# Spreading the first half's inverse roots by two rounded products in a gated convolution layer

## The chip, the cores and the metric

The kernel runs on one core of a Trainium2 chip. Its engines are TensorE (PE in the profile; PEld is its weight load), VectorE (DVE), ScalarE (ACT), GpSimd (POOL), and SyncE (SP), which issues most transfers. Each works through its own queue of instructions in order, and they wait for each other by semaphores. The metric is the device time of one execution in microseconds (us).

## What is computed

One layer with a convolutional mixer (the reference's list of layers has one entry): a sequence of 1024 rows with 1024 channels, all in float32.

```python
def rms_norm(x, g):
    xf = x.astype(jnp.float32)
    y = xf * lax.rsqrt(jnp.mean(xf * xf, axis=-1, keepdims=True) + RMS_EPS)
    return (y * g.astype(jnp.float32)).astype(x.dtype)

def conv_mixer(h, w_in, conv_w, conv_b, ln_g, ln_b, w_out):
    z = h @ w_in
    a, b, gate = jnp.split(z, 3, axis=-1)
    u = a * jax.nn.sigmoid(b)
    u = lax.conv_general_dilated(
        u, conv_w[:, None, :], window_strides=(1,), padding=[(CONV_K - 1, 0)],
        dimension_numbers=("NWC", "WIO", "NWC"), feature_group_count=CONV_WIDTH,
    ) + conv_b
    uf = u.astype(jnp.float32)
    mu = jnp.mean(uf, axis=-1, keepdims=True)
    var = jnp.mean(jnp.square(uf - mu), axis=-1, keepdims=True)
    uf = (uf - mu) * lax.rsqrt(var + LN_EPS) * ln_g.astype(jnp.float32) + ln_b.astype(jnp.float32)
    u = jax.nn.silu(uf).astype(h.dtype) * jax.nn.silu(gate)
    return u @ w_out

# the layer: h + conv_mixer(rms_norm(h, norm_g[0]), ...)
```

`1 / sqrt(mean(x*x) + eps)` of a row is what this text calls the row's inverse root.

## The kernel before

**Layout.** Activations lie with the channels on the 128 partitions (8 groups, index `k`) and the rows along the free axis. The 1024 rows are two halves of 512 (index `h`), each of four tiles of 128 (`TPH`); tiles 0 to 3 are the first half, 4 to 7 the second. The second half is worked on first. Each f32 value of a projection is split into a rounded part (`_hi`, type fp32r) and a remainder (`_lo`), and each product of the projection is three matmuls: hi by hi, lo by hi, hi by lo.

**Projection.** The 24 groups of output channels are "units" (`UNITS`: b and a of a group in turn, then the gate's g). A pass is one unit on one half: 8 `k` times 3 products of 512 columns, 24 in all. The order of passes (`PASSES`) is written out: units 0 and 1 run on raw x (scaled by `norm_g` only) for half 1 and then half 0; then unit 2 and unit 3 on half 0, the same two on half 1, and from unit 4 on each unit on both halves. Half 0 of units 2 and 3 still uses raw x. From unit 2 on half 1 the normalized x is used; its hi part comes from ScalarE (`split_x`, L810), its remainder from GpSimd (`finish_x_lo`, L1427). Behind the projection come the means and deviations of the normalization (L692, L702) and seven output products (L711).

**Inverse roots.** The inverse root of a row stands on the row's partition and has to lie along the free axis, the same on all partitions. ScalarE squares and sums a tile (`square`, L773); GpSimd makes the mean with eps (L1418) and raises it to -0.5 (L1421), for tiles 4 to 7 one at a time, for tiles 0 to 2 together and then tile 3. Then a diagonal matrix of the 128 values is made for each tile, and TensorE multiplies a matrix of ones with it (`spread_rms`). For the second half VectorE makes a rounded and a remainder diagonal for each tile in `diags` (L1086, L1089), and two products of 512 columns add up in one bank (L620, L622). For the first half ScalarE makes four f32 diagonals in `sgate` (`rms_diagonal`, L793), and four f32 products of 128 columns follow (L626). The spread of half 0 stands in unit 3 on half 0 in front of its third `k` (`SPREAD_AT[0] = (3, 0, 2)`).

**Who needs the spread.** ScalarE copies it to SBUF (`copy_rms`, L798), VectorE scales the first units with the copy and makes the normalized x from the spread itself (L1130, L1136, L1098).

**The queues around it.** The order in each queue is written by hand. On ScalarE: squares of tiles 0 to 3 among the splits, `split_x(1, 2)`, the four diagonals, `split_x(1, 3)`, `split_x(1, 4)`, `copy_rms(0)`. On GpSimd: the first weight remainder, two x remainders of half 1, the inverse roots of tiles 0 to 2 and of 3, six more x remainders, the sum of lanes (L1472), the remainder of unit 4's weights (L1438), eight x remainders of half 0, and then the convolution's sums. On VectorE a subtraction of unit 3's weights (L1120, both inputs in SBUF) stands between the normalized x of `k` 5 and 6.

## Time and profile before

| | us |
|---|---|
| median of three runs (363.17 to 363.48) | 363.22 |
| profiled execution, its own time | 363.72 |
| its span | 361.9 |
| TensorE busy | 356.9 |
| VectorE busy | 319.9 |
| GpSimd busy | 269.8 |
| ScalarE busy | 232.4 |

Times in the trace are counted from the start of the span. In a timeline row stand the start, the duration, the engine, the line of the kernel, the operation, what is written and read, and how many instructions are merged in the row; in square brackets the idle time of the engine in front of it and who ended it. Durations on TensorE overlap: products of 512 columns are recorded with 0.39 to 0.40 us each and start 0.23 us apart, so starts are compared, and not durations added up. The 128-column f32 products leave two records each.

### The profile page before, as it was taken

What the parts mean: (1) busy time and instruction counts of PE and PEld (TensorE: products, weight loads), DVE (VectorE), ACT (ScalarE), POOL (GpSimd) and SP (SyncE); (2) the same over time, 40 slices, a digit from 0 to 9 for tenths busy, and PEclk for the clock granted to TensorE, in tenths of its full rate; (3) what the DMA queues carried; (4) which work ended last, traced back from release to release, by engine and by line L of the source; (5) the groups of instructions that cost most, each with busy time, mean ns of one, the idle gap of its engine ahead of it and who ended that gap; (6) DMA issues with size and microseconds to landing.
All of it is one profiled execution on the core that took longest, in us unless ns stands there. A gap on an engine that the chain in (4) does not pass through costs nothing.

```text
span 361.9 us, 4758 instructions
## 1 busy us (share of the span) xinstructions
PE 356.9 (99%) x1564; PEld 289.2 (80%) x1564; DVE 319.9 (88%) x514; ACT 232.4 (64%) x334; POOL 269.8 (75%) x194
## 2 busy tenths in 40 slices
PE   7999999999999999999999999999999999999996
PEld 6888888888888888888888888888888888888885
DVE  4779799999999899999999998993798979997952
ACT  5889685558847772998667875975655951452400
POOL 0029999999999997899999999795796532359220
PEclk9999999999999999999999999999999999999999
DMA  7995011201411311406112214235713695066042
GB/s 260 403 400 206 34 60 58 91 28 58 116 60 53 65 60 58 116 2 116 58 60 51 67 58 80 96 58 103 246 59 117 237 404 173 0 203 205 31 169 92
DMA packets 30520, 43.51 MB, mean 120 GB/s; under 512 B 18336, under 2 KB 18848, under 8 KB 30496
## 3 DMA queue, kind: packets, MB, share of 16 engines
q1 hardware_dynamic: 30352, 43.21, 37.7%
q8 instruction: 12, 0.20, 0.2%
q14 instruction: 12, 0.10, 0.1%
q10 hardware_dynamic: 144, 0.00, 0.0%
HBM read 34.82 MB, written 4.19 MB: 108 GB/s over the span
## 4 chain that ended last, share of the span: by engine, by line
PE 97%; DMA 1%; SPq 0%; ACT 0%; DVE 0%; issue 0%
PE mm L632 68%; PE acc L711 12%; PE mm L711 9%; PE mm L649 6%; DMA raw<-w_in 1%; PE acc L702 0%; PE acc L692 0%; PE acc L626 0%; ACT w_hi L786 0%; DVE nat L1273 0%; SPq L494 0%; SPq L520 0%; PE acc L620 0%; PE acc L622 0%
## 5 line engine op out<-in xcount | busy, mean ns | idle before, releaser
L632 PE MATMUL mm<-x_hi,w_hi 128*128 128x512 f32 x352 | 139.3, 396 | 0.0
L632 PE MATMUL mm<-x_hi,w_lo 128*128 128x512 f32 x352 | 139.0, 395 | 0.0
L632 PE MATMUL mm<-x_lo,w_hi 128*128 128x512 f32 x352 | 139.0, 395 | 0.0
L1185 DVE SCALAR_TENSOR_TENSOR acc<-u,chan,acc 128x512 f32<-128x512 f32 x157 | 110.7, 750 | 0.1
L632 PEld LDWEIGHTS mm<-x_hi,w_lo 128*128 128x128 f32 x352 | 66.1, 188 | 16.0
L632 PEld LDWEIGHTS mm<-x_hi,w_hi 128*128 128x128 f32 x352 | 66.1, 188 | 15.8
L632 PEld LDWEIGHTS mm<-x_lo,w_hi 128*128 128x128 f32 x352 | 66.1, 188 | 15.8
L1494 POOL TENSOR_TENSOR pconv<-pconv,prod 128x512 f32<-128x512 f32 x60 | 77.3, 1312 | 1.3 <-ACT prod L868 1.3
L1185 DVE SCALAR_TENSOR_TENSOR acc<-u,w_sum,acc 128x512 f32<-128x512 f32 x90 | 67.5, 750 | 1.3 <-ACT acc L850 1.1
L868 ACT ACTIVATE prod<-u,chan 128x512 f32<-128x512 f32 x69 | 47.7, 714 | 15.6 <-POOL pconv L1494 14.3
L1438 POOL TENSOR_TENSOR w_lo<-raw,w_hi 128x1024 fp32r<-128x1024 f32 (+1 forms) x21 | 49.7, 2365 | 9.3 <-ACT w_hi L817 9.2
L1494 POOL TENSOR_TENSOR pool_before<-pool_before,prod 128x512 f32<-128x512 f32 x37 | 48.3, 1305 | 1.1
L951 ACT ACTIVATE x_hi<-sgate 128x512 fp32r<-128x512 f32 x28 | 15.9, 624 | 18.2 <-DVE sgate L1261 18.2
L1454 POOL TENSOR_TENSOR wb_lo<-raw,wb_hi 128x1024 fp32r<-128x1024 f32 x6 | 14.5, 2418 | 16.8 <-DVE x_lo L1241 11.4
L711 PE MATMUL acc<-wb_hi,x_lo 128*128 128x512 f32 (+1 forms) x68 | 26.0, 382 | 0.0
L711 PE MATMUL acc<-wb_lo,x_hi 128*128 128x512 f32 (+1 forms) x68 | 25.9, 382 | 0.0
L711 PE MATMUL acc<-wb_hi,x_hi 128*128 128x512 f32 (+1 forms) x68 | 25.9, 382 | 0.0
L868 ACT ACTIVATE prod<-u,w_sum 128x512 f32<-128x512 f32 x30 | 21.4, 714 | 6.6 <-POOL pool_before L1494 6.6
L817 ACT ACTIVATE w_hi<-raw 128x1024 fp32r<-128x1024 f32 x22 | 23.0, 1047 | 2.7 <-PE mm L632 2.1
L1273 DVE TENSOR_TENSOR nat<-acc,nat 128x512 f32<-128x512 f32 (+1 forms) x22 | 13.7, 660 | 8.9 <-PE acc L711 8.9
L894 ACT ACTIVATE sgate<-nat 128x1024 uint16<-128x1024 uint16 x14 | 14.0, 1046 | 11.8 <-POOL nat L1485 8.7
L907 ACT ACTIVATE rows<-sgate 128x1024 uint16<-128x1024 uint16 x14 | 18.2, 1372 | 4.1 <-DMA sgate<-sgate 3.4
(109 smaller groups left out, 541.2 us busy)
## 6 DMA issues: line engine op xcount, KB each, us to landing
raw<-w_in SPq DMA_DIRECT2D x22, 512.0 KB, 3.3
nat<-x_t SPq DMA_DIRECT2D x16, 256.0 KB, 6.1
sgate<-x SPq DMA_DIRECT2D x8, 512.0 KB, 10.8
raw<-w_out SPq DMA_DIRECT2D x8, 512.0 KB, 3.3
nat<-x SPq DMA_DIRECT2D x8, 512.0 KB, 7.9
y<-nat SPq DMA_DIRECT2D x15, 256.0 KB, 2.1
raw_late<-w_out SPq DMA_DIRECT2D x4, 512.0 KB, 4.1
sig<-w_out SPq DMA_DIRECT2D x4, 512.0 KB, 3.9
```

What stands on the lines that cost most here:

```text
L632: ins = nc.tensor.matmul(bank(("unit", m, h)), w[:, m % 3, k, :], xx[:, k, half(h)], start=(k == 0 and i == 0), stop=(k == KC - 1 and i == 2))
L649: return nc.tensor.matmul(bank(("unit", m, h)), w[:, m, k, :], xx[:, k, half(h)], start=(k == 0 and i == 0), stop=(k == KC - 1 and i == 2))
L711: ins = nc.tensor.matmul(product_bank(b, q), v[:, k0 + k, rows], w[:, k, piece_columns(b, q)], start=(k == 0 and i == 0 and continued(b, q ...
L817: nc.scalar.activation(w_hi[:, m % 3, :, :].rearrange("p k n -> p (k n)"), raw[:, m % 2, :], ACT.Copy).then_inc(whi_ready, 1)
L868: nc.scalar.activation(dst, chain_in(j, chain, k), ACT.Identity, scale=tap(j, chain, k), bias=bias(j, chain) if k == 0 else 0.0).then_inc( ...
L894: nc.scalar.activation(planes()[:, i * T:(i + 1) * T].rearrange("p (h s q) -> p h s q", h=NH, s=2), words(nat[:, j, :])[:, :, i].rearrange ...
L907: nc.scalar.activation(words_of_rows(side)[:, :, :, i], crossed()[:, NT * i:NT * (i + 1), :], ACT.Copy).then_inc(rows_joined, 1)
L951: nc.scalar.activation(v_pair(b, k)[0], v_raw(b, k), ACT.Copy).then_inc(vhi_ready, 1)
L1185: ins = nc.vector.scalar_tensor_tensor(dst, chain_in(j, chain, k), tap(j, chain, k), chain_bank(j, chain), ALU.mult, ALU.add)
L1438: nc.gpsimd.tensor_tensor(w_lo[:, m % 3, ks, :].rearrange("p k n -> p (k n)"), raw[:, m % 2, ks.start * P:], w_hi[:, m % 3, ks, :].rearran ...
L1454: ins = nc.gpsimd.tensor_tensor(lo, source, hi.bitcast(F32), ALU.subtract)
L1494: ins = nc.gpsimd.tensor_tensor(pool_sum(chain), summand, prod[:, SLOTTED.index((j, chain, k)) % 4, :], ALU.add)
```

## The change

The first half's inverse roots are treated as the second half's are. GpSimd rounds them to fp32r and subtracts the rounded from the full value (`split_rms`, new, once for tiles 0 to 2 and once for tile 3). ScalarE makes from each part a diagonal, so eight instead of four, and writes them to `diags`, which the second half's spread has used before (hence the wait on `rms_all_ready`). TensorE waits for all eight and issues two products of 512 columns with the rounded ones. The old wait was for each diagonal in turn.

```diff
+        rms_parts = sb("rms_parts", [P, 2, TPH], F32R)
...
-        def diag(i):
-
-            return sgate[:, i, 0:P]
-
...
             def spread_rms(h):

+                spread = rms_spread(h).rearrange("p (t q) -> p t q", t=TPH)
+                pe.wait_ge(ones_r_ready, 1)
                 if h == 1:
-                    spread = rms_spread(1).rearrange("p (t q) -> p t q", t=TPH)
-                    pe.wait_ge(ones_r_ready, 1)
                     pe.wait_ge(diag_hi_ready, TPH)
-                    nc.tensor.matmul(spread, ones_r[:], diags[:, 0, :, :], start=True, stop=False)
+                else:
+                    pe.wait_ge(diag_ready, 2 * TPH)
+                nc.tensor.matmul(spread, ones_r[:], diags[:, 0, :, :], start=True, stop=False)
+                if h == 1:
                     pe.wait_ge(diag_lo_ready, TPH)
-                    ins = nc.tensor.matmul(spread, ones_r[:], diags[:, 1, :, :], start=False, stop=True)
-                else:
-                    for i in range(TPH):
-                        pe.wait_ge(diag_ready, i + 1)
-                        ins = nc.tensor.matmul(rms_spread(0)[:, i * P:(i + 1) * P], ones[:], diag(i), start=True, stop=True)
-                ins.then_inc(rms_all_ready, 1)
+                nc.tensor.matmul(spread, ones_r[:], diags[:, 1, :, :], start=False, stop=True).then_inc(rms_all_ready, 1)
...
             def rms_diagonal(t):

                 act.wait_ge(ident_in, 16)
-                act.wait_ge(rms_ready, rms_count(t))
-                nc.scalar.activation(diag(t), ident[:], ACT.Copy, scale=rms[:, t:t + 1]).then_inc(diag_ready, 1)
+                act.wait_ge(rms_all_ready, 1)
+                for i in range(2):
+                    act.wait_ge(rms_parts_ready, 2 * (rms_count(t) - TPH - 1) + i + 1)
+                    nc.scalar.activation(diags[:, i, t, :], ident[:], ACT.Copy,
+                                         scale=rms_parts[:, i, t:t + 1].bitcast(F32)).then_inc(diag_ready, 1)
...
+            def split_rms(tiles):
+
+                part = slice(tiles[0], tiles[-1] + 1)
+                done = 2 * (rms_count(tiles[0]) - TPH - 1)
+                pool.wait_ge(rms_ready, rms_count(tiles[0]))
+                nc.gpsimd.tensor_scalar(rms_parts[:, 0, part], rms[:, part], 1.0, 0.0, ALU.mult,
+                                        ALU.add).then_inc(rms_parts_ready, 1)
+                pool.wait_ge(rms_parts_ready, done + 1)
+                nc.gpsimd.tensor_tensor(rms_parts[:, 1, part], rms[:, part], rms_parts[:, 0, part].bitcast(F32),
+                                        ALU.subtract).then_inc(rms_parts_ready, 1)
+
...
             inverse_rms(range(TPH - 1))
+            split_rms(range(TPH - 1))
             inverse_rms((TPH - 1,))
+            split_rms((TPH - 1,))
```

On GpSimd, between the x remainders (L1427) and the next six of them, the queue before reads:

```order
L1427 TENSOR_TENSOR x_lo<-nat,x_hi 128x512 [waits xhi_ready] x2
L1418 TENSOR_SCALAR mean_sq<-mean_sq 128x3 [waits sumsq_ready]
L1421 TENSOR_TENSOR rms<-mean_sq,half_neg 128x3 [waits ms_ready]
L1418 TENSOR_SCALAR mean_sq<-mean_sq 128x1 [waits sumsq_ready]
L1421 TENSOR_TENSOR rms<-mean_sq,half_neg 128x1 [waits ms_ready]
L1427 TENSOR_TENSOR x_lo<-nat,x_hi 128x512 [waits xhi_ready] x6
```

The same place in GpSimd's queue now, with the line numbers of the changed kernel:

```order
L1437 TENSOR_TENSOR x_lo<-nat,x_hi 128x512 [waits xhi_ready] x2
L1417 TENSOR_SCALAR mean_sq<-mean_sq 128x3 [waits sumsq_ready]
L1420 TENSOR_TENSOR rms<-mean_sq,half_neg 128x3 [waits ms_ready]
L1428 TENSOR_SCALAR rms_parts<-rms 128x3 [waits rms_ready]
L1431 TENSOR_TENSOR rms_parts<-rms,rms_parts 128x3 [waits rms_parts_ready]
L1417 TENSOR_SCALAR mean_sq<-mean_sq 128x1 [waits sumsq_ready]
L1420 TENSOR_TENSOR rms<-mean_sq,half_neg 128x1 [waits ms_ready]
L1428 TENSOR_SCALAR rms_parts<-rms 128x1 [waits rms_ready]
L1431 TENSOR_TENSOR rms_parts<-rms,rms_parts 128x1 [waits rms_parts_ready]
L1437 TENSOR_TENSOR x_lo<-nat,x_hi 128x512 [waits xhi_ready] x6
```

Four small steps are added, two behind each power, and the six x remainders stand behind them.

On ScalarE, from the third `split_x` (L810) to the copy of the spread (L798), the queue before reads:

```order
L810 ACTIVATE x_hi<-nat 128x512 [waits a_ready,hn_ready]
L793 ACTIVATE sgate<-ident,rms 128x128 [waits rms_ready,ident_in] x4
L810 ACTIVATE x_hi<-nat 128x512 [waits a_ready,hn_ready] x2
L798 ACTIVATE pconv<-acc 128x512 [waits rms_all_ready]
L810 ACTIVATE x_hi<-nat 128x512 [waits a_ready,hn_ready]
```

The same place on ScalarE now (L791 is the diagonal):

```order
L809 ACTIVATE x_hi<-nat 128x512 [waits a_ready,hn_ready]
L791 ACTIVATE diags<-ident,rms_parts 128x128 [waits rms_parts_ready,rms_all_ready,ident_in]
L791 ACTIVATE diags<-ident,rms_parts 128x128 [waits rms_parts_ready]
...
L791 ACTIVATE diags<-ident,rms_parts 128x128 [waits rms_parts_ready,rms_all_ready,ident_in]
L791 ACTIVATE diags<-ident,rms_parts 128x128 [waits rms_parts_ready]
L809 ACTIVATE x_hi<-nat 128x512 [waits a_ready,hn_ready] x2
L797 ACTIVATE pconv<-acc 128x512 [waits rms_all_ready]
```

Eight diagonals stand where four stood, and each waits for its part; the two splits and the copy come behind all eight.

## Rows read from the trace of the kernel before

**Rows 1.** The page, parts 1, 2 and 4: busy time, granted clock, last chain.
```profile
PE 356.9 (99%) x1564; PEld 289.2 (80%) x1564; DVE 319.9 (88%) x514; ACT 232.4 (64%) x334; POOL 269.8 (75%) x194
...
PEclk9999999999999999999999999999999999999999
...
PE 97%; DMA 1%; SPq 0%; ACT 0%; DVE 0%; issue 0%
```

**Rows 2.** Waits of TensorE: us in total, times, longest.
```profile
PE mm L649 <- ACT w_hi L786: 1.2, 1, 1.2
```

**Rows 3.** Timeline of TensorE at the first half's spread: start, duration, instruction.
```profile
36.77 1.05 PE L626 MATMUL acc<-sgate,ones 128*128 128x128 f32 x8
37.58 0.47 PE L632 MATMUL mm<-x_hi,w_hi 128*128 128x512 f32 x1
37.89 0.39 PE L632 MATMUL mm<-x_lo,w_hi 128*128 128x512 f32 x1
```

**Rows 4.** Timeline of TensorE at the second half's spread.
```profile
25.12 0.39 PE L620 MATMUL acc<-diags,ones_r 128*128 128x512 f32 x1
...
25.58 0.40 PE L649 MATMUL mm<-x_hi,w_hi 128*128 128x512 f32 x1
```

**Rows 5.** Timeline of ScalarE, from the diagonals to the copy.
```profile
34.09 1.31 ACT L793 ACTIVATE sgate<-ident,rms 128x128 f32<-128x128 f32 x4
35.31 1.14 ACT L810 ACTIVATE x_hi<-nat 128x512 fp32r<-128x512 f32 x2
37.86 0.60 ACT L798 ACTIVATE pconv<-acc 128x512 f32<-128x512 f32 x1 [1.41 <-PE acc L626]
```

**Rows 6.** Timeline of GpSimd, inverse roots of tiles 0 to 3.
```profile
32.40 0.19 POOL L1418 TENSOR_SCALAR mean_sq<-mean_sq 128x3 f32<-128x3 f32 x1
32.68 0.85 POOL L1421 TENSOR_TENSOR rms<-mean_sq,half_neg 128x3 f32<-128x3 f32 x1
33.75 0.53 POOL L1418 TENSOR_SCALAR mean_sq<-mean_sq 128x1 f32<-128x1 f32 x1 [0.22 <-ACT sgate L773]
34.36 0.55 POOL L1421 TENSOR_TENSOR rms<-mean_sq,half_neg 128x1 f32<-128x1 f32 x1
34.87 3.79 POOL L1427 TENSOR_TENSOR x_lo<-nat,x_hi 128x512 fp32r<-128x512 f32 x3
```

**Rows 7.** Timeline of VectorE beside it.
```profile
33.01 1.22 DVE L1120 TENSOR_TENSOR w_lo<-raw,w_hi 128x1024 fp32r<-128x1024 f32 x1
```

**Rows 8.** Groups of GpSimd by shape: count, busy us, mean ns of one.
```profile
L1438 POOL TENSOR_TENSOR w_lo<-raw,w_hi 128x1024 fp32r<-128x1024 f32 x20 | 48.4, 2418 | 9.3 <-ACT w_hi L817 9.2
...
L1427 POOL TENSOR_TENSOR x_lo<-nat,x_hi 128x512 fp32r<-128x512 f32 x16 | 20.3, 1296 | 0.6 <-ACT x_hi L810 0.6
```

**Rows 9.** Timelines of TensorE and ScalarE at TensorE's one wait.
```profile
7.33 0.50 PE L649 MATMUL mm<-x_hi,w_hi 128*128 128x512 f32 x1 [1.17 <-ACT w_hi L786]
7.67 0.62 PE L649 MATMUL mm<-x_lo,w_hi 128*128 128x512 f32 x2
...
6.65 0.63 ACT L786 ACTIVATE w_hi<-raw 128x512 fp32r<-128x512 f32 x1 [1.57 <-DMA raw<-w_in]
```

**Rows 10.** Timeline of GpSimd, weight remainders of unit 4 and of a later one.
```profile
44.49 2.41 POOL L1438 TENSOR_TENSOR w_lo<-raw,w_hi 128x1024 fp32r<-128x1024 f32 x1 [0.16 <-ACT w_hi L817]
...
145.41 2.41 POOL L1438 TENSOR_TENSOR w_lo<-raw,w_hi 128x1024 fp32r<-128x1024 f32 x1 [3.07 <-ACT w_hi L817]
```

**Rows 11.** Timelines of VectorE, ScalarE and the weight loads near the end.
```profile
259.95 4.87 DVE L1205 TENSOR_TENSOR nat<-nat,acc 128x512 f32<-128x512 f32 x8 [0.51 <-PE acc L692]
...
275.15 0.60 ACT L834 ACTIVATE sgate<-mm 128x512 f32<-128x512 f32 x1 [2.17 <-PE mm L632]
...
276.30 2.50 DVE L1241 TENSOR_TENSOR x_lo<-sgate,x_hi 128x512 fp32r<-128x512 f32 x4 [0.72 <-ACT x_hi L951]
...
285.21 2.49 DVE L1241 TENSOR_TENSOR x_lo<-sgate,x_hi 128x512 fp32r<-128x512 f32 x4
...
285.91 0.19 PEld L711 LDWEIGHTS mm<-wb_hi,x_hi 128*128 128x128 f32 x1
```

More of the change, by code:

```diff
@@ L203, in gated_conv_layer @@
         rms_all_ready = sem("rms_all_ready")
+        rms_parts_ready = sem("rms_parts_ready")
         hn_ready = sem("hn_ready")
```

## The prediction

> **What bounds the kernel now.** I read the page's first and fourth parts before anything else. TensorE is busy for 99% of the span, its granted clock stands at full speed (9 in every slice), and the chain that ended last is 97% TensorE [rows 1]. The list of who waited for whom then says how solid this is: TensorE has one wait of note, 1.2 us near the start [rows 2], and none after it. From 7.33 us on it issues one product behind another. So the time is the sum of TensorE's intervals, and an edit counts only if it shortens that stream or puts a hole into it. The next view is therefore TensorE's timeline around the spread of the first half's inverse roots, then those of the three engines that feed it.
>
> **TensorE: what is removed and added.** The old spread is four f32 products of 128 columns, recorded as eight. They start at 36.77; the first product of the unit that follows is recorded at 37.58 (long, 0.47, as its weights come late) and the second at 37.89 [rows 3]. From the start of the spread to that second product is 1.12 us. The new spread is two products of 512 columns in the rounded form. The second half's spread already is just that, in the same kernel: 25.12 to 25.58 for the two, 0.46 us or 0.23 each, at the pace of the products around them and with their weight loads hidden [rows 4]. From the first of them to that same second product there are three such intervals, 0.69 us. **Term 1: 1.12 - 0.69 = 0.43 us gained**, provided that the operands are there at 36.77.
>
> **Are the operands there?** Before, ScalarE made four diagonals from 34.09 on, ending at 34.09 + 1.31 = 35.40, 1.37 us ahead of their use [rows 5]. Now it makes eight, and TensorE waits for all eight before the first product. ScalarE's next instruction started at 35.31, so a diagonal costs (35.31 - 34.09)/4 = 0.305 us in its queue, and four more cost 1.22 us [rows 5]. With the same start, the eighth begins at 34.09 + 7 x 0.305 = 36.23 and ends 0.39 us later (the first four: 1.31 - 3 x 0.305), at 36.62.
>
> They do not have the same start, since they now wait for GpSimd's two parts. GpSimd ends the power of tiles 0 to 2 at 32.68 + 0.85 = 33.53 [rows 6]. The rounding follows at about 33.62 (these small steps follow each other by 0.08 to 0.09). The step is a copy of the TENSOR_SCALAR at 32.40, which takes 0.19 us; but the same operation at 33.75 took 0.53 and ended at 34.28 [rows 6]. What differs is VectorE: its subtraction of 1024 columns with both inputs in SBUF ran from 33.01 to 34.23 [rows 7]. The short operation ended 0.05 us after it. I take it that the rounding, which starts inside the same stretch, ends at 34.28 too. The Trainium skill states such a rule (SBUF — State Buffer, section "SBUF: two separate sides"): VectorE operations with two SBUF inputs and GpSimd operations that read SBUF take one pair of ports in turn, and the later one is blocked. By this rule the change meets a delay that durations alone do not show, and the row at 33.75 agrees; without the rule the rounding would end at 33.81 and the diagonals would start at 34.09, which is the first rival below.
>
> The first diagonal then starts at about 34.34 instead of 34.09. The remainder is a subtraction of 3 columns. The trace has no such small one; 512 columns take 1.296 us and 1024 take 2.418 [rows 8], so the slope is 2.2 ns a column and the fixed part 0.17 us: about 0.19 us, from 34.36 to 34.55. The far bound above it is the power, 0.85 us for 3 columns and 0.55 for one [rows 6]; the bound below is nothing. I take 0.19, since the subtraction is the same operation as those of rows 8. It is done before ScalarE can start the second diagonal at 34.65. Tile 3 follows on GpSimd: mean at 34.64, power from 34.92 to 35.47, its two parts at 35.75 and 36.03; ScalarE wants them at 36.17 and 36.48. So from 34.34 ScalarE sets the pace: the eighth starts at 34.34 + 7 x 0.305 = 36.48 and ends at 36.87.
>
> **What this does to TensorE.** The trace has one restart after a wait on ScalarE: the activation ends at 6.65 + 0.63 = 7.28, the product starts at 7.33 and the next at 7.67, 0.34 later instead of 0.23, for the weights are then loaded in the open [rows 9]. Here: end 36.87, first new product 36.91, second 37.25, then two intervals of 0.23, so the reference product comes at 37.71, against 37.89. **Term 2: 0.43 - 0.18 = 0.25 us given back. Net 0.18 us earlier.**
>
> **What else is moved.** The four added GpSimd steps, 4 x 0.28 = 1.1 us, and the rounding's blocking put the six x_lo subtractions, before at 34.87 [rows 6], at about 36.1. ScalarE's next two splits move from 35.31 to 36.79. TensorE wants the last x_lo of this half in the pass of unit 2: 18 products of the pass are left at about 37.5, so the next begins at 41.7 and its last k, 21 products on, at 46.6; GpSimd is done at 36.1 + 6 x 1.27 = 43.7. Cover 3 us. The weight remainder behind them starts at about 45.1 instead of 44.49 [rows 10], 0.6 late, and ends at 47.5 for a unit that begins two passes of 24 products after 41.7, at 53. GpSimd then has no gap until it waits 3.07 us for ScalarE at 145.41 [rows 10]; the 0.6 is gone there. Up to then ScalarE and VectorE may see sums 0.6 us late; without that cover it would cost up to 0.6. ScalarE's copy of the spread waited 1.41 us for TensorE and started at 37.86 [rows 5]. Now the second product ends at 37.25 + 0.39 = 37.64 and ScalarE is free at 37.9: no change for VectorE, which waits for that copy. Nothing moves on SyncE's queue. The extra waits on ScalarE are satisfied long before and sit ahead of its own 0.305 pace.
>
> **Does the gain last to the end?** An earlier TensorE gains nothing if it later waits for VectorE. The tightest place is the second output product: its weights are loaded at 285.91, and VectorE's x_lo, wanted there, starts at 285.21 and takes about 0.6 to 0.7 [rows 11]; no slack. But this chain itself hangs on TensorE: VectorE started at 259.95 after 0.51 us of waiting for the spread means, and at 276.30 after 0.72 us behind ScalarE, which at 275.15 had waited 2.17 us for TensorE [rows 11]. A shift of 0.18, or even 0.43, is smaller than each, so they move together. Gain kept.
>
> **The sum.** Span 361.9 - 0.18 = 361.72; 1.82 us of the profiled execution (363.72) lie outside, so 363.54 for it. It was 0.50 above the median 363.22. From the median: 363.04 us. A measurement of this kernel tells 0.2%, 0.73 us, from no change; none of the terms reaches that.
>
> **Rivals.**
> - *No hole.* GpSimd's rounding isn't held up, or the later start is made good. The eighth diagonal ends at 36.62, TensorE could start at 36.66 and the second product is at 37.00, just as in an unbroken stream. Full 0.43: 362.79. For it: VectorE's operation is the only cause I can name, and it is seen once. Against: the 0.53 row.
> - *The operands come too late (slower).* If the small subtractions cost what the power costs, the first remainder is ready at 34.36 + 0.85 = 35.21, the second diagonal starts at 35.28, and the eighth at 37.11, or behind tile 3's remainder at 37.1; it ends at 37.50. Restart at 37.54, reference product at 38.34, 0.45 later than before: 363.67. The point from which it decides: an eighth diagonal ending after 37.05. Against: no other GpSimd addition or subtraction has such a price.
> - *The gain is lost downstream.* TensorE gets to 285.91 early and finds VectorE where it was, for instance because VectorE is 0.6 late after GpSimd and its own wait at 259.95 is used up: 363.22. For: the handoff with no slack. Against: 0.51, 0.72 and 2.17 us of waits on TensorE.
>
> **Chances.** Forecast 0.50, no hole 0.22, lost downstream 0.14, late operands 0.08, something that I don't see 0.06. The three runs of before spread from 363.17 to 363.48, 0.05 under and 0.26 over their median. The range takes forecast, no hole and lost downstream with that spread: 362.79 less 0.05 and a little for rounding, 362.65, to 363.22 plus 0.26, 363.5. Late operands stay out. Every named case lies within 0.2%, so only the unseen part can leave it: faster 0.03, slower 0.04, same 0.93.
>
> **What the profile after would show.** Two products of 0.39 in place of eight; a hole of about 0.15 to 0.25 us ahead of the first, with ScalarE's diagonals as its releaser; eight diagonals at 0.305; the rounding on GpSimd at about 0.6 us for three columns and 0.19 for one, the subtractions at 0.2; VectorE's start at 259.95 some 0.2 earlier. I am wrong if TensorE shows a new wait elsewhere, if the hole is over 0.43, or if the stream behind the spread isn't earlier although the hole is small.

## The result: slower by a third of a per cent

| | before | after |
|---|---|---|
| median, first comparison (7 executions each) | 363.22 us | 364.6 us |
| ratio, 95% interval | | 1.0038 [1.0025, 1.005] |
| median, later comparison (23 and 12) | 363.41 us | 364.32 us |
| ratio, 95% interval | | 1.0032 [1.002, 1.0045] |
| profiled execution, its span | 363.72, 361.9 us | 364.21, 362.1 us |
| time outside the span | 1.75 to 1.88 us | 2.09 to 2.20 us |

The forecast was 363.04 us, with a range of 362.65 to 363.5. The change is 0.9 us slower, to go by the larger comparison: 0.6 us inside the span (medians 361.6 and 362.2) and 0.31 outside it. The time outside the span is an execution's time less the span that its trace covers. The two profiled spans differ by only 0.2 us, since one execution stands for each.

The page of the profile after, parts 1, 2 and 4, answers to [rows 1]:

```profile
PE 357.6 (99%) x1558; PEld 289.1 (80%) x1558; DVE 319.8 (88%) x514; ACT 233.8 (65%) x338; POOL 270.6 (75%) x198
...
PEclk9999999999999999999999999999999999999999
```

TensorE has six instructions fewer, ScalarE and GpSimd four more each, and the granted clock is full in every slice. TensorE is busy for 357.6 us against 356.9 [rows 1], but that line proves nothing by itself: in profiles of kernels that keep the old spread and the time of before it lies anywhere from 356.5 (eight_diags) to 357.8 (all128), with what TensorE waits for in the first 10 us.

TensorE's waits after (engine, line, who ended it, us in total, times, longest), where [rows 2] stood:

```profile
PE acc L753 <- DVE ones L1072: 1.0, 1, 1.0
PE acc L620 <- ACT diags L791: 0.6, 1, 0.6
```

TensorE's timeline after at the spread, which answers to [rows 3]:

```profile
35.85 0.40 PE L628 MATMUL mm<-x_hi,w_lo 128*128 128x512 f32 x1
36.88 0.47 PE L620 MATMUL acc<-diags,ones_r 128*128 128x512 f32 x1 [0.63 <-ACT diags L791]
37.18 0.40 PE L623 MATMUL acc<-diags,ones_r 128*128 128x512 f32 x1
37.42 0.39 PE L628 MATMUL mm<-x_hi,w_hi 128*128 128x512 f32 x1
37.65 0.39 PE L628 MATMUL mm<-x_lo,w_hi 128*128 128x512 f32 x1
```

The restart is at 36.88, forecast for 36.91, and the second product behind the spread at 37.65, forecast for 37.71. Those two numbers held. But TensorE was ready for the spread at 35.85 + 0.23 = 36.08, not at 36.77 as in the profile of before. Counted by starts it came 36.88 - 36.08 = 0.80 us late; the 0.63 in the row is the idle time behind the recorded end of the product before (35.85 + 0.40). It had been 0.69 us ahead since long before: the second half's spread starts here at 24.43, not at 25.12 [rows 4]. That does not come from the change. In the profile of before the stream had waited 1.17 us for its first weights [rows 9]; in this execution they were there sooner.

The three queues that feed the spread, after: ScalarE, GpSimd (answers to [rows 5] and [rows 6]) and VectorE [rows 7]:

```profile
34.27 2.46 ACT L791 ACTIVATE diags<-ident,rms_parts 128x128 fp32r<-128x128 f32 x8 [0.21 <-POOL rms_parts L1428]
36.64 1.14 ACT L809 ACTIVATE x_hi<-nat 128x512 fp32r<-128x512 f32 x2
```

```profile
32.54 0.85 POOL L1420 TENSOR_TENSOR rms<-mean_sq,half_neg 128x3 f32<-128x3 f32 x1
33.49 0.67 POOL L1428 TENSOR_SCALAR rms_parts<-rms 128x3 fp32r<-128x3 f32 x1
34.24 0.19 POOL L1431 TENSOR_TENSOR rms_parts<-rms,rms_parts 128x3 fp32r<-128x3 f32 x1
...
35.43 0.19 POOL L1428 TENSOR_SCALAR rms_parts<-rms 128x1 fp32r<-128x1 f32 x1
35.70 0.19 POOL L1431 TENSOR_TENSOR rms_parts<-rms,rms_parts 128x1 fp32r<-128x1 f32 x1
35.84 1.27 POOL L1437 TENSOR_TENSOR x_lo<-nat,x_hi 128x512 fp32r<-128x512 f32 x1
```

```profile
32.88 1.22 DVE L1119 TENSOR_TENSOR w_lo<-raw,w_hi 128x1024 fp32r<-128x1024 f32 x1
```

The rounding of three columns takes 0.67 us and ends at 34.16, 0.06 behind VectorE's subtraction (32.88 + 1.22 = 34.10); the same step for one column, with VectorE out of the way, takes 0.19. Eight diagonals follow from 34.27 on, 0.30 apart.

What the timeline doesn't show is in the chain of work that ended last (start of a piece, its duration, its instructions). After:

```profile
37.58 221.20 PE mm L628 x948
...
265.17 15.41 PE mm L628 x66
280.58 5.61 PE acc L707 x24
286.19 5.63 PE mm L707 x24
```

Before, in the same view:

```profile
37.82 221.19 PE mm L632 x948
...
265.36 15.34 PE mm L632 x66
280.70 5.60 PE acc L711 x24
286.30 5.60 PE mm L711 x24
```

The stream after is 0.24 us early at 37.58, 0.19 at 265.17 and 0.12 at 280.58, and at 359.3 it is late: each block of 24 products at the end takes 5.62 us in place of 5.60. TensorE does not wait there and its clock is granted in full. The same instructions run 0.3 to 0.5% slower there, while the 948 products of the projection take the same 221.2 us in these two profiles.

### The profile page after: what moved, and what is told of

It is laid out like the page before. It is cut to its first block, busy times and chain, and to the rows that moved or that the text cites. A ratio compares the mean times of both kernels' runs of the same rounds, so it can differ in the third digit from the quotient of the medians.

```text
span 362.1 us, 4755 instructions
## 1 busy us (share of the span) xinstructions
PE 357.6 (99%) x1558; PEld 289.1 (80%) x1558; DVE 319.8 (88%) x514; ACT 233.8 (65%) x338; POOL 270.6 (75%) x198
## 4 chain that ended last, share of the span: by engine, by line
PE 89%; DMA 3%; SPq 3%; POOL 2%; ACT 1%; issue 1%; DVE 1%; ACTq 0%
PE mm L628 66%; PE acc L707 12%; PE mm L707 9%; DMA raw<-w_in 3%; SPq L492 2%; POOL x_lo L1437 1%; ACT diags L791 1%; SPq L488 0%; PE acc L698 0%; PE acc L688 0%; SPq L518 0%; DVE x_lo L1103 0%; POOL w_lo L1444 0%; POOL w_lo L1448 0%; ACT w_hi L816 0%
## 5 line engine op out<-in xcount | busy, mean ns | idle before, releaser
L1504 POOL TENSOR_TENSOR pconv<-pconv,prod 128x512 f32<-128x512 f32 x60 | 78.6, 1350 | 1.3 <-ACT prod L867 1.3
L1504 POOL TENSOR_TENSOR pool_before<-pool_before,prod 128x512 f32<-128x512 f32 x37 | 49.4, 1334 | 1.1
```

Source lines behind the costliest of these rows:

```text
L1504: ins = nc.gpsimd.tensor_tensor(pool_sum(chain), summand, prod[:, SLOTTED.index((j, chain, k)) % 4, :], ALU.add)
```

## The experiments

Theory A is that the new tile of 32 bytes a partition, declared ahead of most tiles, moves their addresses, and TensorE's interval between products depends on these. Theory B is that the wait at the spread (Term 2) was larger than the forecast had it; the expectations call it L. Theory C puts the time down to GpSimd's added work (G in the expectations) or to the semaphore (S). "Before" is the kernel before, run beside each on the same chip (363.34 to 363.5 us each time); n is the number of executions.

| run | median us | n | ratio to before [95%] | span, median | outside the span | block of 24 |
|---|---|---|---|---|---|---|
| again_before | 363.32 | 12 | 0.9999 [0.9987, 1.001] | 361.5 | 1.79 | 5.60 |
| spread_k3 | 363.96 | 12 | 1.0021 [1.0012, 1.003] | 361.8 | 2.15 | 5.62 |
| eight_diags | 363.4 | 12 | 1.0004 [0.9993, 1.0015] | 361.6 | 1.82 | 5.60 |
| hi_only | 361.75 | 6 | 0.9964 [0.9952, 0.9976] | 359.95 | 1.81 | 5.60 |
| pad32 | 363.93 | 11 | 1.0013 [1.0005, 1.0022] | 362.1 | 1.84 | 5.62 |
| pad64 | 360.47 | 6 | 0.993 [0.9911, 0.9949] | 358.65 | 1.80 | 5.60 |
| pad128 | 358.27 | 4 | 0.9854 [0.9834, 0.9874] | 356.45 | 1.79 | 5.44 |
| pad256 | 363.42 | 10 | 0.9996 [0.9984, 1.0008] | 361.6 | 1.83 | 5.60 |
| out128 | 360.62 | 4 | 0.9922 [0.9906, 0.9938] | 358.8 | 1.81 | 5.44 |
| all128 | 363.24 | 10 | 0.9995 [0.9986, 1.0004] | 361.4 | 1.84 | 5.60 |
| after_end | 363.33 | 12 | 1.0004 [0.9986, 1.0023] | 361.2 | 2.12 | 5.60 |
| after64 | 361.42 | 12 | 0.9958 [0.9942, 0.9973] | 359.3 | 2.13 | 5.60 |
| after128 | 359.52 | 5 | 0.9885 [0.9865, 0.9905] | 357.4 | 2.13 | 5.44 |
| after_again | 364.32 | 12 | 1.0032 [1.002, 1.0045] | 362.2 | 2.12 | 5.62 |
| pool_split_only | 360.82 | 9 | 0.9945 [0.9927, 0.9962] | 358.7 | 2.14 | 5.60 |
| pool_four | 363.54 | 12 | 1.0 [0.999, 1.0011] | 361.45 | 2.11 | 5.60 |
| sem_only | 363.38 | 12 | 0.9996 [0.9983, 1.0009] | 361.55 | 1.80 | 5.60 |
| used_sem | 363.39 | 10 | 0.9993 [0.9975, 1.0011] | 361.55 | 1.79 | 5.60 |

### The spread itself

**again_before** is the kernel before, unchanged.

> The kernel before, unchanged, with a profile of its own. The two profiles so far differ in where TensorE stands when it reaches the spread: 36.77 us before, 36.09 us (35.85 + 0.23) in the changed kernel, where it then waits 0.63 us for ScalarE's diagonals. Theory L (late operands): TensorE usually arrives at about 36.1, as it did after, and the 36.77 came from a late first weight piece (its wait of 1.17 us for ScalarE at 7.33). Then this profile shows the spread at 36.0 to 36.4 in most executions, and a time of 363.0 to 363.5. Theory P (the change itself makes TensorE arrive earlier): the spread again at 36.7 to 36.8. The share of the time outside the span was 1.82 us before and 2.1 in the changed kernel; if that is the change's, it is 1.8 here.

At 363.32 us the time fits either theory; the place of the spread fits neither (36.0 to 36.4 for L, 36.7 to 36.8 for P). Its profile shows the same kernel 0.42 us later at the spread than the first profile of before did [rows 3]:

```profile
37.19 1.05 PE L626 MATMUL acc<-sgate,ones 128*128 128x128 f32 x8
...
38.00 0.47 PE L632 MATMUL mm<-x_hi,w_hi 128*128 128x512 f32 x1
38.31 0.39 PE L632 MATMUL mm<-x_lo,w_hi 128*128 128x512 f32 x1
```

The profiled executions of kernels that leave the front of the program and its tiles as they were reach the spread between 36.15 (out128) and 37.19, a range of 1.0 us, and the forecast had used one value of it. The first weights are not the only reason: here the product behind the first weights starts at 7.33 and the second half's spread at 25.12, both as in the first profile [rows 9, rows 4], and the 0.42 us are lost between 26.97 and 27.86, where products start 0.54 and 0.35 us apart and not 0.23.

**spread_k3** puts the changed spread one `k`, three products, later.

```diff
-SPREAD_AT = {1: (0, 4), 0: (3, 0, 2)}
+SPREAD_AT = {1: (0, 4), 0: (3, 0, 3)}
```

> The changed kernel with the first half's spread one k (three products, 0.70 us) later in the pass of unit 3, everything else the same. Theory L: the hole of 0.63 us is covered by three products, so the stream behind it is 0.6 us earlier than in the changed kernel, about 364.0, or some 0.8 us above the kernel before, whose four f32 products it would beat by 0.43 otherwise; the rest must then lie outside the spread. If the hole is the only loss, it is 0.4 us under the kernel before: 362.8. Theory G (GpSimd's shifted queue costs it): no change against the changed kernel, 364.6.

TensorE does not wait any more:

```profile
36.80 0.40 PE L628 MATMUL mm<-x_hi,w_lo 128*128 128x512 f32 x1
37.14 0.48 PE L620 MATMUL acc<-diags,ones_r 128*128 128x512 f32 x1
```

The time came as expected (363.96 for 364.0). The span is 0.4 us shorter than that of the changed kernel in after_again (361.8 against 362.2). So the wait is real and costs about 0.4 us, and it is not the whole: without it the kernel is still 0.21% slower than before [0.12, 0.30].

**eight_diags** keeps the old products and adds only the four further diagonals, for all of which TensorE waits.

```diff
-                        pe.wait_ge(diag_ready, i + 1)
+                        pe.wait_ge(diag_ready, 2 * TPH)
...
+                act.wait_ge(rms_all_ready, 1)
                 nc.scalar.activation(diag(t), ident[:], ACT.Copy, scale=rms[:, t:t + 1]).then_inc(diag_ready, 1)
+                nc.scalar.activation(diags[:, 1, t, :], ident[:], ACT.Copy, scale=rms[:, t:t + 1]).then_inc(diag_ready, 1)
```

> The kernel before, with eight diagonals on ScalarE instead of four (the second of each pair is not used) and TensorE waiting for all eight before its four f32 products; GpSimd is unchanged. Theory L: the eighth diagonal ends at 36.62 less 0.1, so TensorE, arriving at 36.1, waits 0.4 to 0.5 us: 363.6 to 363.7. Theory G: as the kernel before, 363.2.

One wait of 0.21 us in its profile (TensorE came at 36.39), and no difference in time that can be told: 363.4, under the 363.6 to 363.7 of Theory L. ScalarE's part alone is nearly free.

**hi_only** makes four rounded diagonals and one product of 512 columns; the remainders are left out.

```diff
-                    for i in range(TPH):
-                        pe.wait_ge(diag_ready, i + 1)
-                        ins = nc.tensor.matmul(rms_spread(0)[:, i * P:(i + 1) * P], ones[:], diag(i), start=True, stop=True)
+                    spread = rms_spread(0).rearrange("p (t q) -> p t q", t=TPH)
+                    pe.wait_ge(ones_r_ready, 1)
+                    pe.wait_ge(diag_ready, TPH)
+                    ins = nc.tensor.matmul(spread, ones_r[:], diags[:, 0, :, :], start=True, stop=True)
...
-                nc.scalar.activation(diag(t), ident[:], ACT.Copy, scale=rms[:, t:t + 1]).then_inc(diag_ready, 1)
+                act.wait_ge(rms_all_ready, 1)
+                nc.scalar.activation(diags[:, 0, t, :], ident[:], ACT.Copy, scale=rms[:, t:t + 1]).then_inc(diag_ready, 1)
```

> The kernel before, with four rounded diagonals on ScalarE and a single product of 512 columns; GpSimd unchanged. The remainders of the inverse roots are left out. The product costs one interval of 0.23 us where the four f32 products cost 0.89, and the diagonals end at 35.4 as before, ahead of TensorE in any case. Theory L and the first term of my sum: 0.66 us under the kernel before, 362.55. If the first term is wrong (a faster spread on TensorE is not passed on to the end): 363.2.

```profile
36.74 0.39 PE L627 MATMUL acc<-diags,ones_r 128*128 128x512 f32 x1
36.97 0.39 PE L633 MATMUL mm<-x_hi,w_hi 128*128 128x512 f32 x1
37.20 0.39 PE L633 MATMUL mm<-x_lo,w_hi 128*128 128x512 f32 x1
```

From the spread to the second product behind it 0.46 us, where the four old products took 1.12 [rows 3]: each rounded product costs the 0.23 of Term 1, and the open weight load at 37.58 is gone. The rest of its 1.6 us was not expected. In its chain the 948 products of the projection take 220.29 us, against 221.19 in the first profile of before. But so they do in other profiled executions with no tile moved, again_before (220.30) and after_end (220.30), while sem_only and pool_four show 221.19 and 221.20. With these addresses the interval has two values, 0.2324 and 0.2333 us, and no run here shows what chooses; even an execution at 0.2333 does its last 66 projection products at 0.2324 (15.34 us). The 0.66 of the products and those 0.9 make the 1.6 between the two profiles (360.3 and 361.9 us). That the 0.9 stands behind the medians too is not shown, since the interval is known for profiled executions alone.

### What the new tile moves

**pad32** is the kernel before with nothing but an unused tile of 32 bytes where the change declares `rms_parts`.

```diff
         half_neg = sb("half_neg", [P, NT])
+        pad = sb("pad", [P, 2, TPH], F32R)
         stats = sb("stats", [P, NT, KC // 2, 6])
```

> The kernel before with one unused tile of 32 bytes a partition at the place of the new rms_parts, and nothing else; all tiles allocated behind it (w_hi, w_lo, u, the output weights) lie 32 bytes further. In the chain of work the changed kernel and spread_k3 take 5.62 us for 24 output products and 221.2 for the 948 of the projection; the kernel before takes 5.60, and 220.3 or 221.2 in its two profiles. Theory A (address): 5.62 here too and 221.2, so 0.3 to 1.2 us over the kernel before, 363.7 to 364.5, with 1.8 us outside the span. Theory S (the semaphore or the queues): as the kernel before, 363.35, 5.60.

```profile
37.64 221.21 PE mm L633 x948
...
265.24 15.41 PE mm L633 x66
280.65 5.61 PE acc L712 x24
286.26 5.63 PE mm L712 x24
```

The blocks are at 5.62 us, and the median rises by 0.59 us (by the interval of the ratio, 0.2 to 0.8) with not one instruction added. Theory A holds for this part. Against the first profile of before, the chain places 0.34 us of it: 0.07 in the run of 66 products and 0.27 in the output. A further part may be that the interval of 0.2324 is gone: all four profiles with 32 bytes more (after, after_again, spread_k3, pad32) show 0.2333 in the projection, where four of those with unmoved tiles have 0.2324. That part is not shown.

**after64** is the changed kernel with a tile of 64 bytes in place of 32 (`[P, 4, TPH]`).

> The changed kernel with rms_parts made 64 bytes a partition instead of 32 (the second half of it unused), so that the tiles behind it move by another 32 bytes. Theory A: 24 output products in 5.60 us again, and the projection's 948 in 220.3 in at least part of the executions: 0.3 to 1.2 us under the changed kernel, 363.4 to 364.3; the hole of 0.6 us at the spread and 2.15 us outside the span stay. Theory S: no change, 364.6.

It came at 361.42, 2 us under the expectation. The output blocks are at 5.60 as Theory A has it, but the projection's products start 0.2289 us apart, closer than in the kernel before or after.

**after_end** is the changed kernel with its own tile declared last in the first stage, so that no other tile moves.

```diff
-        rms_parts = sb("rms_parts", [P, 2, TPH], F32R)
...
+            rms_parts = sb("rms_parts", [P, 2, TPH], F32R, first)
```

> The changed kernel with rms_parts allocated as the last tile of the first stage, so that every other tile stands where it stood before the change. The sum of what the runs have shown of the changed kernel against the kernel before: the hole less the faster products (0.63 - 0.43 = 0.2), the time outside the span (0.35), and the addresses (pad32: 0.6). Theory A with these sizes: 0.6 us under the changed kernel, 364.0, with 24 output products in 5.60 us. If the position of rms_parts doesn't matter: 364.6 and 5.62.

The expectation missed: it is as fast as before (ratio 1.0004 [0.9986, 1.0023]), 0.7 us under what was expected. Together with after_again this is the second proof for the tile: the same instructions are 0.9 us slower than before with the tile ahead of the others and even with before with the tile behind them. Blocks are back at 5.60, and the median span is 0.4 us below before's. The wait is there, but shorter, since TensorE came at 36.64:

```profile
37.13 0.47 PE L620 MATMUL acc<-diags,ones_r 128*128 128x512 f32 x1 [0.33 <-ACT diags L791]
```

**pad64, pad128 and pad256** are pad32 with a larger tile: 64, 128 and 256 bytes.

> The kernel before with one unused tile of 64 bytes a partition where the changed kernel has rms_parts, and nothing else. after64 and pool_split_only, which move the tiles by these 64 bytes, took 217 us for what takes 220.3 to 221.2, and then waited for VectorE at the spread of the means. Theory A: this comes from the addresses alone, so the span is that of pool_split_only, 358.6, with 1.8 us outside it: 360.4, 0.8% under the kernel before. If it needs GpSimd's steps as well: 363.35.

> As pad64, with 128 bytes. The projection's product intervals so far: 0.2324 or 0.2333 us with the tiles where they are, 0.2333 moved by 32 bytes, 0.2289 moved by 64. If what matters is where the weights lie within 128 bytes, this is as the kernel before, 363.35. If it is within 256 or more, it is another value, either way. The output products stay at 5.60 for 24 in either case, as only the 32-byte shift has changed them.

> The kernel before with an unused tile of 256 bytes a partition at the place where the changed kernel declares its new tile. Theory 1, that the interval falls with each 64 bytes and repeats after 256: back to 0.2333 us and 363.4. Theory 2, that the product is fastest where some tile's start is a multiple of 128 or more, as 128 bytes happened to make it: the same. Theory 3, that it goes on falling with distance: 0.225 us or less in the projection, and under 357 us. The two first are told from the third by over 5 us.

64 bytes came out as expected (360.47 for 360.4). 128 came out 5 us below the kernel before, a value that the expectation had left open, and its output blocks fell to 5.44 where it had them stay at 5.60. 256 is back at the start, as if the effect repeated; that is one point. The windows of TensorE show it without any chain (stretch, busy time and number of instructions of each engine, then the granted clock and DMA's share). Before:

```profile
40.00:250.00 210.00, 210.00 (x902) 168.95 (x901) 203.54 (x321) 150.71 (x209) 198.91 (x142) 1.00 0.25 66
280.00:350.00 70.00, 70.00 (x301) 56.30 (x301) 63.36 (x91) 30.83 (x45) 32.75 (x14) 1.00 0.51 180
```

pad128:

```profile
40.00:250.00 210.00, 210.00 (x928) 173.88 (x927) 202.56 (x320) 151.54 (x211) 198.28 (x142) 1.00 0.24 67
280.00:350.00 70.00, 70.00 (x310) 58.00 (x309) 62.59 (x89) 27.51 (x40) 29.36 (x13) 1.00 0.51 183
```

Both are at full clock and 100% busy; in the same 210 us one gets through 902 products and the other through 928. "Busy 99%" was no proof that the stream could not be faster.

In pad64 and pad128 TensorE becomes fast enough to wait for someone else, VectorE's variances (in pad128 VectorE itself stood 5.9 us for ScalarE's rows, L926, just before them). TensorE's waits in pad128, and the stretch behind the wait:

```profile
PE acc L693 <- DVE mean_var L1200: 2.2, 1, 2.2
```

```profile
255.00:259.50 4.50, 4.50 (x22) 3.92 (x22) 4.46 (x12) 3.06 (x3) 3.79 (x4) 0.62 0.77 279
```

After that 2.2 us of standing the granted clock averages 0.62 for 4.5 us, that is, most of the stretch at the lower level of 1.2 GHz. In after128 the wait was 2.8 us and the profiled execution stayed at full clock. The executions without a profile show the same two cases by their mean granted clock: pad128 has a span of 355.0 us at 1.0 and 356.3 to 356.7 at 0.995 (three of four executions), pad64 358.3 to 359.2 and once 360.4 at 0.994. In the kernels where TensorE does not wait at the variances the mean is 0.999 or more, but for two executions of the kernel before, with spans of 364.0 and 364.3 us. So the medians of pad64 and pad128 already contain part of this loss.

**out128 and all128** place the 128 bytes elsewhere: out128 ahead of the output weights `wb` alone, all128 ahead of the very first tile, x.

```diff
         wb = {}
+        pad = sb("pad", [P, 32])
         for slot in (3, 0, 1, 2):
```

```diff
+        pad = sb("pad", [P, 32])
         nat = sb("nat", [P, NT, D])
         x_hi = sb("x_hi", [P, KC, T], F32R)
```

> The kernel before with an unused tile of 128 bytes a partition ahead of the output weights' tiles (wb) alone; all tiles of the projection stay where they were. What tells the theories apart is whether the interval of the products goes with the addresses of what each stage's own products read. If it does (theory 1), the projection keeps 0.2324 to 0.2333 us a product (some 220 to 221 us for its 948 products) and the output blocks of 24 products fall from 5.60 to 5.44 us: over some 17 blocks 2.5 to 3 us, so 360.6 us and a ratio near 0.992. If the 128 bytes acted through something else that moved with them in the first stage, such as the tiles that ScalarE, VectorE and GpSimd use (theory 2), the blocks stay at 5.60 and the time at 363.4.

> The kernel before with the unused 128 bytes ahead of the very first tile, so that every tile moves by the same distance, x and its remainders too. If the absolute addresses of the weights decide (theory 1), the interval is as with 128 bytes ahead of the weights: 0.2267 us and 5.44 us a block, 358.3 us, ratio 0.986. If the distance between the two operands of a product decides (the weights against x, theory 2), nothing is changed by this: 0.2333 us, 5.60 us and 363.4.

The chain of out128 shows both stages side by side:

```profile
37.20 221.19 PE mm L633 x948
...
264.73 15.34 PE mm L633 x66
280.07 5.45 PE acc L712 x24
285.52 5.44 PE mm L712 x24
```

The projection is untouched and the output blocks are at 5.44: each stage goes by its own tiles. In all128, where all tiles move by the same 128 bytes, nothing changes (all128, 363.24 us):

```profile
37.48 221.19 PE mm L633 x948
...
280.35 5.60 PE acc L712 x24
```

So it isn't the absolute address that counts but the distance, and what the weights of both stages are at a distance from is x, whose parts are the other operand of every product (in the output it lies in x's tiles too). But in pad128 other tiles of the first stage move along with its weights, in out128 `spare` and `raw_late` move along with `wb`, and x is not the only tile that stays, so it is not proved that the pair of operands does it. By what mechanism the distance sets the interval is not shown at all.

### The time outside the span

**sem_only, used_sem and pool_split_only**: a semaphore that nobody uses; one that VectorE signals once, by an added write of one column, and GpSimd waits for; GpSimd's four steps of the change with their semaphore and a tile of 64 bytes, their results unused.

> The kernel before with one semaphore more, which nothing uses. The time outside the span was 1.76 to 1.87 us in 29 executions of the kernel before and 2.11 to 2.2 in 19 of the two kernels with rms_parts_ready. Theory S: 2.15 here, so 0.35 us over the kernel before, 363.7. If only a semaphore that is waited on costs it, or the GpSimd instructions do: 1.8, 363.35. The chain of work as before (5.60).

> The kernel before with one semaphore more that is raised once by an added VectorE memset of one column and waited on once by GpSimd at the start, where it is long raised. The three kernels with rms_parts_ready have 2.08 to 2.20 us outside the span, the others 1.76 to 1.88, the one with an unused semaphore among them. Theory S2 (a semaphore in use costs it): 2.15 outside, 363.7. Theory I (GpSimd's added instructions cost it): 1.8, 363.35.

> The kernel before with GpSimd's four added steps and their semaphore, their tile 64 bytes wide; nothing reads the two parts, and ScalarE and TensorE work as before. GpSimd's x remainders and what follows are 1.1 us later. Theory G: this later queue costs up to 0.6 us. Theories L, A and S together: the span as before (TensorE without a new wait, 5.60 us for 24 output products) and only the time outside it longer, 2.15: 363.7.

**pool_four** adds four GpSimd instructions and nothing else.

```diff
+            scratch = sb("scratch", [P, 8], F32, first)
...
+            for i in range(4):
+                nc.gpsimd.tensor_scalar(scratch[:, i:i + 1], half_neg[:, 0:1], 1.0, 0.0, ALU.mult, ALU.add)
```

> The kernel before with four GpSimd instructions more, at the place where the change puts its four steps: each takes one column of a constant tile and writes one column of an unused tile that is declared last in the first stage, so that nothing else moves. No semaphore, no wait and no other engine is involved, and GpSimd's 0.8 us more are absorbed as in the run with the split alone. Theory 1, that the time outside the span goes with GpSimd's added instructions: 2.08 to 2.20 us outside the span instead of 1.76 to 1.88, and 363.4 + 0.33 = 363.75 us in all, ratio 1.001. Theory 2, that it goes with what the change's instructions do (their type, or the semaphore between them): 1.8 us outside, and 363.4.

The semaphores leave the time outside the span at 1.8 us. Every kernel with the four GpSimd instructions has 2.11 to 2.15, those of pool_four included, which wait for nothing. The 0.31 us go with the instructions. Why is open. pool_four's time as a whole rises by only 0.13 (ratio 1.0000 [0.999, 1.0011], under the 363.75 of its expectation), as its span is 0.15 under before's; that the whole 0.31 us reach the total is seen in pool_split_only, 360.82 against pad64's 360.47 with the same span.

In pool_split_only GpSimd's next steps are late by 1.1 us, as the forecast had it, and the time does not show it: its span equals that of pad64 (358.7 and 358.65). The expected 363.7 was missed by 2.9 us, because its tile of 64 bytes moved the others.

### Does it add up, and is the change worth anything elsewhere?

> The changed kernel again, unchanged, for more executions of it. By the parts found so far: the kernel before with the 32 bytes alone is at 363.93, the time outside the span adds 0.33, and the spread gives -0.45 for its products and +0.3 to +0.65 for its wait, so 364.1 to 364.5. If it is at 364.7 or more, the parts do not add up to it and something of 0.3 us or more is missing from the account. The interval between products should be 0.2333 us in the projection and the output blocks 5.62 us, the wait at the spread 0.3 to 0.8 us, and the time outside the span 2.08 to 2.20 us.

It came at 364.32, within the 364.1 to 364.5. Its span is 362.2, that of pad32 362.1.

**after128** is the changed kernel with a tile of 128 bytes.

> The changed kernel with its new tile enlarged to 128 bytes, so that the other tiles lie as in the kernel before with an unused 128 bytes (358.27). It asks what the change itself is worth where addresses cost nothing. There TensorE waited 2.2 us for the normalization's variances, which VectorE ends. If the spread's 0.43 us counts and that wait does not take it: about 358.3 - 0.43 + 0.2 to 0.6 for the wait in front of the spread + 0.35 outside the span = 358.4 to 358.7. If VectorE's end at the variances sets the time (it stands at the same place whatever TensorE does), the gain is lost there: 358.3 + 0.35 = 358.6, with the wait longer by what TensorE gained. A time of 358.0 or less would say that the change is worth its 0.43 us.

At 359.52 (0.8 us over the top of its expectation) it beats the kernel before by 1.15%, but not pad128 (358.27), which has the same addresses and the old spread. At like clock the order is the same: 356.1 and 356.5 us of span against 355.0 at full clock, 357.4 to 358.3 against 356.3 to 356.7 at 0.995. At 64 bytes it is alike: 361.42 against 360.47. In both pairs 0.33 us of the difference (0.95 and 1.25 us) lies outside the span. Inside it TensorE waited 0.77 us at the spread in after128, since it was ready there at 36.16, ahead of the diagonals:

```profile
37.09 0.47 PE L620 MATMUL acc<-diags,ones_r 128*128 128x512 f32 x1 [0.77 <-ACT diags L791]
```

In these kernels TensorE waits for the variances, and that wait ends at 255.46 us in after128 and at 254.05 in pad128. The 1.4 us are there early: VectorE starts its work on the spread at 38.57 against 37.70, and GpSimd its weight remainder at 45.08 against 43.62. Which of the two carries it to the variances is open; between pad64 and after64 GpSimd is late by 1.3 us too (44.08 and 45.41), and yet the wait for the variances ends only 0.06 us apart (256.40 and 256.46). after128 has 5 executions and pad128 4.

pad128 is the fastest kernel of the study: one unused tile of 128 bytes, 1.46% [1.26, 1.66] below before. The change adds 1.25 us to it.

## Why the prediction was wrong

**The pace of the new products: right.** Term 1 took 0.23 us each and no open load behind them: 37.18 and 37.42 after, 36.74 and 36.97 in hi_only.

**The feeding queues: right.** The rounding was foretold at 33.62 to 34.28 and ran to 34.16, held up by VectorE. The forecast's reading of 0.53 us [rows 6] decided here over the sum of durations: 0.67 us beside VectorE and 0.19 without. The Trainium skill's rule (SBUF — State Buffer, section "SBUF: two separate sides") has the later of two such operations blocked for the whole of the earlier one. The trace agrees for the rounding and not for VectorE: its subtraction began at 32.88 us while GpSimd's power ran from 32.54 to 33.39, and took 1.22 us all the same. GpSimd's subtraction took 0.19, the diagonals 0.30 each, GpSimd came to its x remainders at 35.84 (forecast 36.1) and to the weight remainder at 44.87 (45.1). The remainder for tile 3 was ready well in time. Neither the first rival (no hole) nor the second (an eighth diagonal after 37.05; it ended at 36.73) came true. In after64 the eighth ended at 37.20, but there the whole front of the execution was 0.5 us later, and the subtraction took 0.19 as elsewhere.

**The step that failed first: "provided that the operands are there at 36.77".** TensorE's arrival was read from one execution, in which it had waited 1.17 us for its first weights [rows 9], and that wait was even used for another purpose in the forecast, as the price of a restart. The restart depends on ScalarE, the arrival on waits further up TensorE's own stream; so Term 2 is whatever lies between two moments that don't move together. Counted as the forecast counted it, arrival to second product less the 0.69 of an unbroken stream, Term 2 was 37.65 - 36.08 - 0.69 = 0.88 us in the profile after, 37.67 - 36.29 - 0.69 = 0.69 in after_again, and 37.91 - 36.64 - 0.69 = 0.58 in after_end, where the forecast had 0.25. That is 0.3 to 0.6 more and takes all of Term 1: between pad32 and after_again, which differ by the change without its address effect, the spans differ by +0.1 us instead of -0.18. From after_end it would be -0.4, in a set of executions where the interval of 0.2324 may have been commoner; the spread's net is known no better than between these.

**"1.82 lie outside", taken unchanged: wrong.** It became 2.12, 0.31 us, since GpSimd has four instructions more. Of this nothing in the trace of before could tell.

**The cause that was missing: the tile's declaration.** It stands in the first line of the diff and the forecast costed it at nothing, without a sentence. It is the largest single part: 0.59 us by pad32 (0.2 to 0.8 by its interval), and 1.0 us by the step from after_end (0.1 below before) to after_again (0.9 above it). The 0.06 given to what is not seen was too little for a change that adds a tile ahead of nearly all others.

**The sum.** Inside the span +0.6 from addresses and about +0.1 from the spread with its wait, outside it +0.31: 1.0 us, against 0.91 measured in the second comparison (364.32 - 363.41). This is no independent check, since the 0.1 was itself read from after_again less pad32.

**Downstream: the forecast's claim is untested in part.** In the profile after TensorE waits nowhere behind the spread, so nothing was lost there; but there was no gain to be lost either. Where TensorE did gain, in pad64 and pad128, VectorE's variances became a wait of 2.0 and 2.2 us, at a place that the forecast had not looked at (it looked at 259.95 and 285.91 [rows 11]). At the variances after128 waits 0.6 us longer than pad128, and its wait ends 1.4 us later.

## What to carry to other kernels

A gain on the bounding engine that needs its operands sooner has to be set against the earliest arrival of that engine in several executions, not against that of one profile. A change that declares a tile moves all tiles behind it: run the old kernel with nothing but the empty tile beside the new one, and declare the new tile last. And before tuning instructions of a kernel whose TensorE is 99% busy, try paddings of 32 to 256 bytes ahead of the weights, since here an empty tile did more than any other edit, for better (128 bytes) and for worse (32).

## What the runs showed of the hardware

**The interval between TensorE's products of 512 columns in fp32r depends on where the tiles lie.** By bytes added between x and the weights, us per product (from starts in the timeline and from the pieces of the chain), and in the second row the whole run as the chain has it:

| bytes | 0 | 32 | 64 | 128 | 256 |
|---|---|---|---|---|---|
| projection (L632), mean between 40 and 240 us | 0.2324 or 0.2333 | 0.2333 | 0.2289 | 0.2267 | 0.2333 |
| end of the projection, a run of 66 products | 15.34 | 15.41 | 15.11 | 14.98 | 15.34 |
| output (L711), a block of 24 products / 24 | 0.2333 | 0.2342 | 0.2333 | 0.2267 | 0.2333 |

At 256 bytes it is back where it was, and moving x along undoes it. In the output stage 64 bytes do nothing and 128 give all; in the projection 64 give a good half. The unpadded distance of the two stages may differ, so the columns aren't the same distances for both rows.

**Four small GpSimd instructions more lengthen the time outside the span by 0.3 us** (2.11 to 2.15 against 1.79 to 1.84), in seven kernels out of seven that have them and in none of the eleven others. No run here shows the reason.

**Behind a wait of about 2 us TensorE's granted clock fell in some executions and not in others.** In pad128 TensorE had stood for 2.2 us, and the clock then averaged 0.62 between 255.0 and 259.5 us; after128 stood for 2.8 us and kept 1.00. Executions of pad128 with a mean clock of 0.995 are 1.3 to 1.7 us longer than the one at 1.0.
